# A streaming encoder step on eight cores: the third tile's first norm transposed by DMA instead of TensorE

## What is computed

```
h = rmsnorm(x, g1); z = h @ w_in            # 1024 -> 1536 = [pool | u | v]
a = z[:512]; u, v = gelu(z[512:1024]), gelu(z[1024:])
pool: trailing means of a (windows 2/4/8/16) minus a, per-group 128x128 map, per-channel scale
gmlp: u * (W_s v + b) over 128-position chunks, block-causal mask
x = x + concat(pool, gmlp) @ w_out
f = rmsnorm(x, g2) @ w_up                   # 1024 -> 4096
x = x + relu(f)^2 @ w_down                  # 4096 -> 1024
y = rmsnorm(x, gf)
```

## Time and profile before

| what | us |
|---|---|
| runs | 1255.3, 1258.23, 1363.93 (median 1258.23) |
| profiled execution | 1256.96 |
| its span, slowest core (6) | 1255.4 |
| spans of the eight cores | 1252.5 to 1255.4 |
| PE busy | 1231.0 (98%) |
| DVE, ACT, POOL busy | 542.9, 378.0, 53.2 |

### The profile page before, as it was taken

One profiled execution on the slowest core, in us unless ns is written; L12 is line 12 of the kernel. 1 busy time (PEld: TensorE's weight loads), 2 busy tenths in 40 slices (PEclk: granted clock), 3 DMA queues, 4 the chain that ended last, 5 costly groups with the idle time before them and its releaser, 6 DMA issues.

```text
span 1255.4 us, 20126 instructions; the slowest of 8 cores (1252.5 to 1255.4 us)
## 1 busy us (share of the span) xinstructions
PE 1231.0 (98%) x7009; PEld 680.1 (54%) x7068; DVE 542.9 (43%) x1324; ACT 378.0 (30%) x738; POOL 53.2 (4%) x102
## 2 busy tenths in 40 slices
PE   6899999999999999999999999999999999999997
PEld 3555655555555654655565465556546555654554
DVE  3875543335455640661364066136406613530413
ACT  3644321134313430441243044124304412330412
POOL 4000000001100100100010010001001000000000
PEclk9999999999999999999999999999999999999999
DMA  9999558938954675567458556646855665775752
GB/s 195 175 232 167 142 128 165 212 118 279 300 176 126 182 238 202 191 175 221 168 185 235 201 194 172 222 168 185 235 201 192 184 212 171 126 227 202 251 202 85
DMA packets 89034, 239.85 MB, mean 191 GB/s; under 512 B 55747, under 2 KB 56003, under 8 KB 66406
## 3 DMA queue, kind: packets, MB, share of 16 engines
q1 hardware_dynamic: 74592, 182.73, 45.6%
q0 software_dynamic: 13760, 54.95, 20.7%
q10 hardware_dynamic: 582, 0.86, 0.2%
HBM read 213.69 MB, written 34.43 MB: 198 GB/s over the span
## 4 chain that ended last, share of the span: by engine, by line
PE 95%; DMA 2%; issue 1%; DVE 1%; ACT 0%; SPq 0%; ACTq 0%; DVEq 0%
PE ps L943 35%; PE ps L985 29%; PE ps L897 9%; PE ps L758 9%; PE ps L973 7%; PE ps L781 4%; DMA HT<-HB 1%; DMA PWF<-ident 1%; PE ps L608 1%; PE ps L857 1%; DVE HB L594 0%; PE ps L497 0%; PE ps L478 0%; ACT JUNK L543 0%; SPq L601 0%
## 5 line engine op out<-in xcount | busy, mean ns | idle before, releaser
L943 PE MATMUL ps<-H2T,RING 128*128 128x384 bf16 x2816 | 463.3, 326 | 0.0
L985 PE MATMUL ps<-RING,ST 128*128 128x512 bf16 (+1 forms) x1723 | 371.7, 375 | 1.9
L943 PEld LDWEIGHTS ps<-H2T,RING 128*128 128x128 bf16 x2816 | 274.9, 98 | 181.0 <-issue 0.2
L985 PEld LDWEIGHTS ps<-RING,ST 128*128 128x128 bf16 x1760 | 172.1, 98 | 199.0
L947 ACT ACTIVATE ST<-ps 128x384 bf16<-128x384 f32 x352 | 171.1, 489 | 312.3 <-PE ps L943 312.2
L543 ACT ACTIVATE JUNK<-X 128x1024 bf16<-128x1024 f32 (+3 forms) x104 | 106.3, 1022 | 427.1 <-DVE X L993 321.0
L949 DVE TENSOR_TENSOR ST<-ST 128x384 bf16<-128x384 bf16 x352 | 124.4, 356 | 221.9 <-ACT ST L947 220.7
L993 DVE TENSOR_TENSOR X<-ps,X 128x512 f32<-128x512 f32 x99 | 68.4, 690 | 324.6 <-PE ps L985 285.9
L758 PE MATMUL ps<-HT,WIN 128*128 128x384 bf16 x640 | 106.5, 326 | 0.0
L758 PEld LDWEIGHTS ps<-HT,WIN 128*128 128x128 bf16 x640 | 62.5, 98 | 41.6
L973 PE MATMUL ps<-RING,ST 128*128 128x512 bf16 x375 | 82.9, 379 | 0.5
(11 more groups left out here) (127 smaller groups left out, 503.9 us busy)
## 6 DMA issues: line engine op xcount, KB each, us to landing
RING<-scr SPq DMA_DIRECT2D x144, 1024.0 KB, 5.0
scr<-RING SPq DMA_DIRECT2D x16, 1024.0 KB, 12.1
X<-xall POOLq DMA_DIRECT2D x30, 512.0 KB, 6.9
yall<-X POOLq DMA_DIRECT2D x30, 512.0 KB, 4.3
RING<-w_up POOLq DMA_DIRECT2D x8, 1024.0 KB, 13.7
RING<-w_down POOLq DMA_DIRECT2D x8, 1024.0 KB, 14.0
WIN<-w_in POOLq DMA_DIRECT2D x6, 512.0 KB, 21.4
X<-xall SPq DMA_DIRECT2D x3, 512.0 KB, 6.8
```

The source lines that it names most:

```text
L943: i_ = e.matmul(bank(ub)[:, 0:TOK], lhsT=RING[s][:, k, m4 * 128:(m4 + 1) * 128], rhs=H[:, k, :], start=(k == 0), stop=(k == 7))
L985: i_ = e.matmul(bank(fb)[:, 0:c1 - c0], lhsT=ST[:, kg * 8 + kk, n * 128:(n + 1) * 128], rhs=RING[s][:, kk, c0:c1], start=(kg == first and ...
```

## The change

The first tile whose transposes go by DMA becomes tile 2, but only for its first norm: the second keeps its PE transposes and ACT copies. The DMA transposes of tile 2's first norm are marked `slow`, and the planner counts every successor of a marked operation as ready 40 us after its planned landing (if the successor's priority isn't negative). Nothing else differs in the program; the order on all engines is planned anew.

```diff
-DMA_T0 = 3
+DMA_T0 = 2
+SLOW_T = 40.0
@@ class Op
         self.nbytes = 0
+        self.slow = False
@@ schedule, done
                     elif op.nbytes and s.eng in ("act", "dve"):
                         late = LOAD_MARGIN
+                    if op.slow:
+                        late = SLOW_T
                 s.ready = max(s.ready, t + late)
@@ norm_T
-        def norm_T(hb, dstT, dst_res, ncol0, name=None):
+        def norm_T(hb, dstT, dst_res, ncol0, name=None, slow=False):
             if name is not None:
-                add("sp", lambda e: e.dma_start_transpose(out=dstT[:, :, ncol0:ncol0 + 128], in_=HB[hb][:]),
+                op = add("sp", lambda e: e.dma_start_transpose(out=dstT[:, :, ncol0:ncol0 + 128], in_=HB[hb][:]),
                     reads=[("HB", hb)], writes=[dst_res], dma=name)
+                op.slow = slow
                 return
@@ tr_items
-                name = None if i < DMA_T0 else f"tr{kind}_{n}" if kind == "1" else f"tr2_{i % 2}_{n}"
+                name = None if i < DMA_T0 or (i == 2 and kind == "2") else f"tr{kind}_{n}" if kind == "1" else f"tr2_{i % 2}_{n}"
                 if kind == "1":
-                    norm_T(hbs[("1", i)][n], h1(i)[0], h1res(i, n), n * 128, name)
+                    norm_T(hbs[("1", i)][n], h1(i)[0], h1res(i, n), n * 128, name, i == 2)
                 else:
-                    norm_T(hbs[("2", i)][n], H2T[i % 2], ("H2T", i % 2, n), n * 128, name)
+                    norm_T(hbs[("2", i)][n], H2T[i % 2], ("H2T", i % 2, n), n * 128, name, i == 2)
```

## The result

The changed kernel takes 1269.61 us in the median of 22 runs, against 1256.88 for the kernel before (22 runs); the ratio is 1.007, 95% interval 1.0045 to 1.0095. By that ratio it is slower by some 9 us, where 1.35 us less had been forecast, and the time lies above the stated range. The ratio leaves out disturbed executions, and with them five (1274.36 to 1295.96 us) in which single cores were late in the same way as in the others, so it rather understates the loss: the medians are 12.7 us apart. The profiled execution spans 1263.5 us on its slowest core.

A forecast was written before the change was run, and what follows sets the result against it. PE was taken as the bound, busy 1231.0 of 1255.4 us. From the profiled execution's 1256.96 us, 1.35 us of PE transposes came off and all other terms counted 0, giving 1255.6 us; range 1252.0 to 1263.0.

The forecast's parts named there:

- The gain: On PE, tile 2's first norm loses three groups of eight transposes, 3 x 0.45 = 1.35 us, all on the path.
- The order: On PE, tile 2's a/u projections move from 131.02 to 209 to 225 us; only another order of work, cost 0.
- the side work: Tile 2's a/u projections through last norm-2 transpose, 48.3 us, end at 257 to 273 us, before its MLP; cost 0.
- Rival (b): Tile 2's side work comes too late for its MLP: 1261 to 1276 us, 1265 as middle; chance 0.12.
- its point of 282.6: Time in us beyond which tile 2's last norm-2 transpose must lie for rival (b) to hold (285.5 - 2.9).
- DMA time added: Three DMA transposes beside the casting loads add 10.5 us of DMA time, below 27 us slack; cost on PE 0.
- the upper end of 3 x 14.6: Upper bound of added DMA time, three slowest landings, 44 us, of which 17 us would reach PE (rival c).
- The two rows behind it: Later tiles' transpose landings (3.0 to 14.6 us, median 3.5) and DMA shares of 0.92 and 1.66 at 400 us.
- 27 us of slack: Slack of GpSimd's ring loads: PE wants the chunk 41 us after issue, and a load lands in 13.1 us.
- The step beside it: Two new waits, DVE's block 2 apply and PE's projections for HT, bite only beyond 40 us lateness; taken as 0.
- Rival (c): Transposes among casting loads take 14.6 us each, PE waits for ring chunks: up to 17 us, 1257 to 1273; chance 0.05.

The follow-up runs named there:

- the run with the order alone: Changed kernel with tile 2's first norm back on PE transposes and ACT copies, successors still planned 40 us late: 1255.94 us, ratio 0.9992 to the kernel before.

## Why the prediction was wrong

*The gain was sized rightly.* The PE transposes fell from 144 to 120 and 3 x 0.45 us came off wherever the DMA held: from the mark to tile 2's MLP, 179.08 us on five cores against 180.42 before. The kernel that keeps the transposes apart gives 2.5 us (1.3 to 3.8), whose interval just holds the 1.35.

*The order was read rightly.* The a/u projections stood at 221.10 us on core 1, within 209 to 225, tile 2's MLP began at 283.23 (forecast 285.5, for a core that reached the mark 2.3 us later), and PE took a chunk every 10.4 us without starving: the run with the order alone has 0.9992. Where the transposes came in time, the side work fitted. Rival (b) didn't happen. On core 3 the last norm-2 transposes slid to 281.99 us, close to its point of 282.6, but the MLP slid with them, to 296.25, so its margin was untouched.

*The step that failed* is "DMA time added": "I take 3 x 3.5 = 10.5 us, by the median ... cost on PE 0", with the upper end of 3 x 14.6. In place of 0, PE of the slowest core lost 11.0 us, 8.2 waiting for the third transpose and 2.7 at the lower clock behind the wait. The two rows behind it belong to tiles 3 to 10, where no casting load is in flight. In the casting stretch one transpose landed in 58.6 us instead of 3.5, and the median of three was 29.9 to 31.2 us on cores 3, 6 and 7. It was mis-sized in kind as well: I added landings up as traffic that takes turns in a queue, and weighed them against 27 us of slack of loads that I left at 13.1 us. But the transposes slow the loads and stores themselves: core 3's loads of w_up took 28.4 us and its stores 30.4, and that ate the slack from the other side. And PE seems to need the DMA for more than data: core 5's 4.5 us fit no term of the sum.

*The step beside it* fell with it: "Both would bite only if a landing were more than 40 us later than planned; the slowest row is 14.6". Once 58.6 us is possible, the 40 us are no cover, and by the planning I had described myself (the lateness counted twice) the third transpose stands where PE takes chunks without a break. The prediction saw that place and priced it at 0.

*Rival (c)* named the right place, transposes among casting loads, and a price of up to 17 us, but not the way the loss took: it had PE waiting for ring chunks, and no core of the changed kernel's profile does. Cores 3 and 6 wait for the transposed block and core 5 for neither; only with two transposes more does PE wait for a chunk. That 11.0 us lies within its 17 is partly luck. I gave it 0.05, on a mean DMA share of 0.60 from 126 to 204 us. That row is of the old order, in which the loads pause; with the late order and no DMA transpose the share there is 0.84 to 0.87, without a loss. So the row said little about the new order, and the full queue was needed for the loss but not enough for it.

A rule of the Trainium skill that I set aside ("Advanced Engine Details and Errata", X-Bar Transpose: transposing DMAs are as fast as regular ones) would have misled as well. In the casting stretch plain copies of the same bytes landed in 5.9 to 10.2 us (medians by core), the transposes on cores 3, 5, 6 and 7 in 18.4 to 31.2, though on the other four in 8.1 to 11.8. With the casting loads held off, 3.3 us were measured.

## What to carry to other kernels

Price a transfer by rows from a stretch with the same traffic; if there is none, the row of a quiet stretch is a lower bound, and the first experiment is one look at the landings, core by core. A DMA transpose is cheap where the load queues have gaps, and dangerous amid loads that keep them full: give it a gap with two dependencies (after one load has landed, before the next is issued). Here that cost nothing, and together with a buffer of its own for the third block it turned a loss of 0.7% into a gain of 0.2% (0.3% with both norms). Compare cores and versions from a mark that lies before the change: the spread of the start hides 1.3 us in the spans, and this distance showed it on every core that had no loss. A planned lateness only hides a late landing; it moves work, and every buffer that is reused behind the transfer counts it once more.

## What the runs showed of the hardware

With a DMA transpose beside two full queues of 1 MB loads and stores, a core's DMA moved 53 GB/s for 8 us where an undisturbed core moved 243, with packets of the casting queue at 6.7 us in the mean, and this happened on some cores and not on others in one execution (four of eight in the profiled one of the changed kernel, three with all three transposes in the early place, two with all in the later). Halving the loads ended it, with the cast or without, and so did keeping loads and transposes apart. Whether the cast or GpSimd's queue is needed, which part of the DMA engines stalls, and why core by core, isn't shown by any run here; that the transposes do it, and plain copies of the same shape and place don't, is. A core whose DMA is slowed can also stop PE within a group of matmuls with no semaphore open: all four such waits of 3.8 to 5.9 us (one in the changed kernel, three with all transposes in the later place) hold a packet of the instruction queue that comes some 2 us before PE goes on. That the instructions came late is the likely reading, not a tested one.
